# Interleaved output classes for dilation 16, strided q and k writes, and a new spread of the memory tasks in a planned encoder block

## The reference, cut to what matters

```
h = rms_norm(x); proj = h @ w_in                       # 9728 columns
A: for g, (window, r) in enumerate(((128,1),(512,4),(2048,16))):
     q = rms_norm(q_g) ; k = rms_norm(k_g)             # per head of 64
     split positions into r residue classes t = c + r*i
     in a class: banded attention, |i_q - i_k| <= 64, ALiBi  -> p (unnormalised), denom
   y_dil = sum_g p_g v_g / sum_g denom_g               # 8 heads, merged by denominators
B: y_ret = bidirectional retention (2 pairs of heads), group norm, silu gate
C: y_mem = cross-attention of 4 heads of 128 into 256 memory tokens
x += (sum_b sigmoid(gate_b) * (y_b @ w_branch_b)) @ w_out
x += (gelu(conv3(u)) * gate) @ w_ffn_out,   [u | gate] = rms_norm(x) @ w_ffn_in   # 2816 wide
```

## Time and profile before

| | us |
|---|---|
| median of 3 runs | 5511.06 (5508.02 to 5718.92) |
| profiled execution | 5508.4 |
| its span on the slowest core | 5506.9 |
| spans of the 8 cores | 5492.7 to 5506.9 |
| TensorE busy | 5232.7 (95%) |
| VectorE busy | 3263.9 (59%) |
| ScalarE busy | 2553.2 (46%) |
| GpSimd busy | 639.5 (12%) |
| mean granted clock of TensorE | 0.99 |

### The profile page before, as it was taken

How to read it: one execution, slowest core, us unless ns; L and a number is a source line. 1 busy time by engine, 2 the same in 40 slices (tenths; PEclk the granted TensorE clock), 3 DMA queues, 4 the chain that set the end, 5 groups by cost and what they waited for, 6 DMA issues and landing times.

```text
span 5506.9 us, 92875 instructions; the slowest of 8 cores (5492.7 to 5506.9 us)
## 1 busy us (share of the span) xinstructions
PE 5232.7 (95%) x33264; PEld 2716.6 (49%) x33264; DVE 3263.9 (59%) x4171; ACT 2553.2 (46%) x4313; POOL 639.5 (12%) x630
## 2 busy tenths in 40 slices
PE   7999999999998899999999889999999989999999
PEld 4555444444555444444455544444445654444444
DVE  4777645663388764566337875466534786546651
ACT  6768523332476852332247685233225668423320
POOL 1211110000111120000011212000001121100000
PEclk9999999999999999999999999999999999999999
DMA  7322446325522152622652215262265221436223
GB/s 142 36 26 21 58 42 142 43 37 172 87 21 28 18 67 33 148 39 37 176 81 24 26 16 67 33 153 39 32 183 73 24 26 17 65 41 146 39 43 115
DMA packets 535777, 360.10 MB, mean 65 GB/s; under 512 B 326816, under 2 KB 476832, under 8 KB 535328
## 3 DMA queue, kind: packets, MB, share of 16 engines
q0 software_dynamic: 458544, 175.27, 28.4%
q1 hardware_dynamic: 76784, 178.88, 9.9%
HBM read 460.13 MB, written 68.16 MB: 96 GB/s over the span
## 4 chain that ended last, share of the span: by engine, by line
PE 80%; DVE 7%; ACT 5%; issue 5%; DMA 2%; POOL 0%; DVEq 0%; SPq 0%; ACTq 0%; POOLq 0%
PE ps L432 79%; ACT arena L450 5%; DVE arena L458 4%; PE ps L436 1%; DVE arena L468 1%; DVE arena L1057 1%; DMA arena<-x 1%; DVE arena L481 1%; DMA arena<-w_in 1%; DMA arena<-mem 0%; ACT arena L454 0%; DMA out<-arena 0%; DVE arena L475 0%; ACT L450 0%; DMA arena<-out 0%
## 5 line engine op out<-in xcount | busy, mean ns | idle before, releaser
L432 PE MATMUL ps<-hT,arena 128*128 128x512 bf16 x13312 | 3088.6, 381 | 54.4 <-ACT arena L454 14.4
L432 PEld LDWEIGHTS ps<-hT,arena 128*128 128x128 bf16 x13312 | 1281.3, 98 | 1533.4 <-issue 118.0
L432 PE MATMUL ps<-arena 128*128 128x512 bf16 (+8 forms) x10784 | 1749.8, 314 | 114.6 <-DVE arena L458 49.3
L458 DVE TENSOR_TENSOR arena<-arena,ps 128x512 f32<-128x512 f32 (+1 forms) x1248 | 918.1, 767 | 1055.8 <-PE ps L432 835.1
L450 ACT ACTIVATE arena<-ps 128x512 bf16<-128x512 f32 (+4 forms) x1488 | 971.5, 676 | 1018.8 <-PE ps L432 999.6
L450 ACT ACTIVATE arena<-arena 128x512 f32<-128x512 f32 (+4 forms) x1008 | 791.2, 799 | 1039.2 <-DVE arena L468 559.8
L432 PEld LDWEIGHTS ps<-arena 128*128 128x128 bf16 (+2 forms) x10784 | 814.1, 98 | 922.8 <-issue 235.1
L458 DVE TENSOR_TENSOR arena<-arena 128x512 bf16<-128x512 f32 (+4 forms) x1082 | 868.6, 815 | 281.6 <-ACT arena L450 234.2
L432 PE MATMUL ps<-arena,hT 128*128 128x128 bf16 (+1 forms) x7168 | 595.3, 230 | 8.9 <-DVE arena L1057 3.4
L432 PEld LDWEIGHTS ps<-arena,hT 128*128 128x128 bf16 x7168 | 525.6, 117 | 126.5 <-issue 26.1
L502 POOL DMA_DIRECT2D arena<-w_in x264 | 235.2, 903 | 2151.8 <-PE ps L432 1776.4
(11 more groups left out here) (45 smaller groups left out, 1220.0 us busy)
## 6 DMA issues: line engine op xcount, KB each, us to landing
arena<-w_in POOLq DMA_DIRECT2D x256, 256.0 KB, 6.5
arena<-x SPq DMA_DIRECT2D x128, 512.0 KB, 5.5
arena<-w_ffn_in POOLq DMA_DIRECT2D x88, 512.0 KB, 7.9
out<-arena SPq DMA_DIRECT2D x64, 512.0 KB, 7.8
arena<-out SPq DMA_DIRECT2D x128, 256.0 KB, 3.4
out<-arena SPq DMA_DIRECT2D x128, 256.0 KB, 2.4
arena<-w_ffn_out POOLq DMA_DIRECT2D x16, 1024.0 KB, 14.6
arena<-w_in POOLq DMA_DIRECT2D x8, 1024.0 KB, 11.1
```

The costliest lines, as they stand in the source:

```text
L432: return lambda e: e.matmul(out, lhsT=lhsT, rhs=rhs, start=st, stop=sp)
L458: return Op("vector", [lambda e: e.tensor_tensor(out=out, in0=in0, in1=in1, op=op)], rd, wr, 0.157 + _n(out) / (1920.0 if fast else 960.0) ...
```

## The change

Five edits, all in the order or the form of existing operations; no product or sum of the reference is added or left out.

1. For r = 16 the matmuls of `d_pv` write their 128 words with a stride of 4, so that the 4 classes of a bank lie interleaved; the addition reads the bank in order and the accumulator in runs of 4 adjacent words, 16 words apart.
2. The last product of `d_qk` walks in token order: both f32 inputs are read without gaps and the bf16 store is written with the stride of a class (2048/r elements).
3. The scaling at L1057 may also go to ScalarE, as an activation with a scale; the copy of g = 0 in `ev_gen` may too.
4. The memory tasks' priorities go from 300 + 9k to 220 + 17k (k = 0 to 15).
5. A token `Omm` tells that all 16 output projections have their matmuls planned. `f_g(0)` waits for it, and `f_u(1)` waits for it in place of all of `f_u(0)`.

The planner's cost of the addition of g = 1 rises by 0.4 (its own unit, written as `more`), which moves the order alone.

```diff
-def TT(out, in0, in1, op, rd, wr, fast=False):
+def TT(out, in0, in1, op, rd, wr, fast=False, more=0.0):
     return Op("vector", [lambda e: e.tensor_tensor(out=out, in0=in0, in1=in1, op=op)], rd, wr,
-              0.157 + _n(out) / (1920.0 if fast else 960.0), 0.06)
+              0.157 + more + _n(out) / (1920.0 if fast else 960.0), 0.06)
...
-            sc.lane("M", [(T0 + 300 + 9 * (4 * h + tt), m_task(h, tt)) for h in range(4) for tt in range(4)], 3)
+            sc.lane("M", [(T0 + 220 + 17 * (4 * h + tt), m_task(h, tt)) for h in range(4) for tt in range(4)], 3)
...
-                yield Op("vector", [lambda e: e.tensor_scalar(out=qf.ap, in0=bk.ap[:], scalar1=pcol(gcol), scalar2=None, op0=ALU.mult)],
-                         bk.keys + ["par"], qf.keys, 0.69, 0.06)
+                yield (Op("vector", [lambda e: e.tensor_scalar(out=qf.ap, in0=bk.ap[:], scalar1=pcol(gcol), scalar2=None, op0=ALU.mult)],
+                          bk.keys + ["par"], qf.keys, 0.69, 0.06),
+                       ACT(qf.ap, bk.ap[:], AF.Copy, bk.keys + ["par"], qf.keys, scale=pcol(gcol)))
...
-                yield GTT(dv_[:, :, i0:i0 + ni], qf.ap.rearrange("p (i c) -> p c i", c=r), rb.ap.rearrange("p (i c) -> p c i", c=r), ALU.mult,
-                          qf.keys + rb.keys, dk_)
+                yield GTT(dv_[:, :, i0:i0 + ni].rearrange("p c i -> p i c"), qf.ap.rearrange("p (i c) -> p i c", c=r),
+                          rb.ap.rearrange("p (i c) -> p i c", c=r), ALU.mult, qf.keys + rb.keys, dk_)
...
                         if g == 0:
-                            yield VCOPY(avs[hh], views[hh], bn[hh].keys, acck[hh])
+                            yield EVICT(avs[hh], views[hh], bn[hh].keys, acck[hh])
                         else:
-                            yield TT(avs[hh], avs[hh], views[hh], ALU.add, bn[hh].keys + acck[hh], acck[hh])
+                            yield TT(avs[hh], avs[hh], views[hh], ALU.add, bn[hh].keys + acck[hh], acck[hh], more=0.4 if g == 1 else 0.0)
...
-                            yield PE([f_mm(bn[hh].ap[:, k4 * 128:(k4 + 1) * 128], dv[:, cl + k4, vsl[hh]], pv[hh][:, k4 * 128:(k4 + 1) * 128], True, True)
+                            yield PE([f_mm(bn[hh].ap[:].rearrange("p (i k) -> p k i", k=4)[:, k4, :], dv[:, cl + k4, vsl[hh]], pv[hh][:, k4 * 128:(k4 + 1) * 128], True, True)
                                       for k4 in range(4)], [128] * 4, pcur.keys + dvk, bn[hh].keys)
...
-                        yield SPAWN(pr, ev_gen(bn, [bn[h].ap[:].rearrange("p (k i) -> p k i", k=4) for h in range(2)],
-                                               [acc[h].rearrange("p (i c) -> p c i", c=r)[:, cl:cl + 4, :] for h in range(2)], pre))
+                        yield SPAWN(pr, ev_gen(bn, [bn[h].ap[:].rearrange("p (i k) -> p i k", k=4) for h in range(2)],
+                                               [acc[h].rearrange("p (i c) -> p i c", c=r)[:, :, cl:cl + 4] for h in range(2)], pre))
...
                     yield UNREF("w", b, "o%d" % hf)
+                yield CNT(16, "Omm", b)
...
-                if j > 0:
+                if j == 1:
+                    yield WAIT("Omm", b)
+                if j > 1:
                     yield WAIT("u", b, j - 1)
...
-                if j > 0:
+                if j == 0:
+                    yield WAIT("Omm", b)
+                else:
                     yield WAIT("u", b, j)
```

## The result

| | us |
|---|---|
| two runs of the changed kernel | 5611.51, 5613.78 |
| ratio to the kernel before | 1.0189, 95% interval 1.0164 to 1.0213 |
| profiled execution, its span | 5613.78, 5612.2 |

The forecast was 5415 with a range of 5340 to 5495. The changed kernel has 5601.

A forecast was written before the change was run, and what follows sets the result against it. Bound by TensorE, busy 5232.7 of 5506.9 us, its idle time mostly in attention, following the busier of VectorE and ScalarE. Attention -83, clock -6, junction -21, interleaved bank +14: -96 from 5511.06, 5415 us; range 5340 to 5495.

The forecast's parts named there:

- the price of the strided write: Last product of q and k: 0.2 us gained each, bounds 0.41 and 0; 11 us off VectorE in 1508:1832.
- each strided stream costs about 0.2: Last product of q and k: one reading of its 1.10 us, by which one strided write leaves 0.89.
- any strided stream costs all 0.41: Last product of q and k: the other reading, by which the strided write gains 0 against today's 1.10 us.
- the clock: Granted clock won back: 1.5 x 4 = -6 us in attention, plus half of the 3.4 us loss at each junction.
- the interleaved bank: 512 matmuls of d_pv at r = 16, slowed from 0.056 to 0.109 us: +27 us, half in idle time, so +14.
- The junction: Output to up projection: earlier f_u(1) closes 3.65 us of holes and half the clock loss; -21 us, bounds 0 and -28.
- the first hole: Output to up projection: TensorE's 2.17 us idle before the last transposes, claimed to close.
- the third hole: TensorE's 2.66 us idle at 2343, waiting for a copy of ScalarE; claimed to stay.
- The additions: Attention, g = 2: 0.687 us for 1.053 each, 16 in 1508:1832, 5.9 us off VectorE.
- The -83 us in attention: Four attention stretches: -20.7 x 4, from 19.1 us less TensorE idle and 1.6 by the memory tasks, per sequence.
- VectorE's relief: Stretch 1508:1832: VectorE's work from 270.6 to 221 us by additions, products, scalings and copies; TensorE idles 12.9 for 32.0.
- the priorities: Memory tasks: last ones give way more, lowering ScalarE's 90% in 1832:1904 towards 84%; -1.6 us, bounds -3.2 and +3.

The follow-up runs named there:

- additions by reads: Kernel before, order kept; the r = 16 addition reads an unbroken bank with a stride of 128 words, accumulator in runs of 4: 5473 us, ratio 0.9956.
- reads of PSUM: Strided PSUM reads making every class order: in the kernel before 5430 us (-69); in the changed kernel, replacing edits 1 and 2, 5401 us (-99).

## Why the prediction was wrong

**The step that failed** is the price of the strided write: "the bounds are a gain of 0.41 and of 0 each (a loss is excluded as far as the additions show, which write with a stride at no more than 1.10)". The additions write f32. The new output is bf16, and no row of before had a 2-byte element written with a gap. It took 2.44 us for 1.10: a loss of 1.34, outside the bounds. Edit 2 alone shows it (+210 us), and taking it out of the changed kernel gives back 179.

The reasoning between the bounds was wrong too: it weighed "each strided stream costs about 0.2" against "any strided stream costs all 0.41". One strided read takes 1.04 us, two take 1.05 and one strided f32 write 1.02 to 1.07, for 0.68 to 0.69 unbroken, so the second was right, and even an f32 output would have gained next to nothing.

**The Trainium skill** (SBUF — State Buffer, Door 1: The DMA port swizzle) was quoted for lines of 16 bytes. For additions in runs of 4 words it held (0.680). For one element per line it gave the sign of "pays", and I turned that into 0 gain instead of asking what a 2-byte write pays. The same page of the Trainium skill puts how far one can stride for free at 4 f32 and 8 bf16; there the runs differ, and the measurement decides: f32 with stride 4 takes 1.07, bf16 with stride 4 takes 1.30 and with stride 8 takes 2.42.

**What held.** Without edit 2 the changed kernel came to 5422 us in span, 77 under the kernel before; the forecast was 96 under it, with 11 us of VectorE's work per sequence laid on edit 2. By terms: TensorE's waits fell by 73 us, where the forecast had 97 (20.7 and 3.65 us a sequence); the clock gave back 28, where it had 13; the interleaved bank was put at +14 on the path, at the pace of 256 columns (0.104 to 0.109 us measured), and costs 18 beside the additions by reads, or 22 to 29 in the table's rest. So the 77 hold a clock term that was half its size and a gap term that was too small as well. The rule of the Trainium skill on gaps in PSUM (PSUM — Partial Sum Buffer, Specifications (TRN2)) agrees for matmuls that write single words; reads with a stride and writes in runs of two words show no such cost here. The junction was put at -21 with a bound of -28; edit 5 alone gave -29. In its trace the second sequence's junction keeps 0.44 us of the first hole, has neither of the others, and runs at a granted clock of 1.00 where it was 0.51; the prediction had counted half of that clock and left the third hole open. The additions fell to 0.68 as forecast.

**What held only by its sum.** The -83 us in attention were laid on VectorE's relief. Edit 3, the largest part of that relief, gave 8 us alone; TensorE waited as long as before (258 us for 260), so the step from the engines' shares to idle time does not hold here. (A slip beside it: the 48.8 us of scalings are 47.8 in the earlier trace rows, which moves nothing.) The order gave more than forecast: 22 us by the priorities, where I had -1.6 a sequence and a mechanism that does not take place, and 20 by the cost of g = 1, which the sum left out. With edits 3 and 5 these add up to -79, and -66 were measured together. That this sum came near the forecast is in part luck. The reads of PSUM took about as much off VectorE as edit 3 alone (2958.5 us busy for 3087.1 in the new order), by making instructions shorter instead of moving them, and gave more: 69 in the old order, and in the new one 33 more than edits 3, 4, 5 and the cost. Why edit 3 is worth 8 us in one setting and 25 in another stays open.

## What to carry to other kernels

Before a permutation is moved from an operand to another, ask which memory, which direction and which element size it meets: the same class order took 1.10 us as a strided f32 read and 2.44 as a strided bf16 write, and as a strided read of PSUM no more than unbroken (the products then took 0.73 on average). A bound taken from rows holds only for their element size; where no row has the new one, leave that side open. A busy share of 76% before and 75% after says nothing of instructions that became longer one by one. And where a change opens or closes waits of TensorE, look at the mean granted clock too: of edit 2's 210 us an estimated 72 were clock.

## What the runs showed of the hardware

Writes to SBUF pay by the distance of their elements, and 2-byte elements more: bf16 at 4, 8 and 16 bytes takes 0.73, 1.30 and 2.42 us for 128x512, f32 at 8 and 16 bytes 0.69 and 1.07, unbroken writes 0.68 and 0.69. On ScalarE a bf16 write with stride 16 takes 2.33 for 0.60 unbroken. Runs of 2 adjacent bf16 with a gap as long as the run were free (0.69), and so were the additions in runs of 4 f32 (0.68). Strided reads of PSUM were free for VectorE and ScalarE (0.75, 0.60 and 0.69), while matmuls that wrote single words with gaps went at 0.109 us for 0.056, and runs of two words restored the pace (0.059). The mean granted clock fell where TensorE waited more: 0.978 with 409 us of waits, 0.985 with 318, 0.995 with 187; but it is not a matter of the sum alone, since edit 4 alone and the cost alone have 250 and 249 us of waits at 0.994 and 0.990.
